# A tuned two-block transformer kernel: last tile in halves and quarters, a new order of the opening loads, and the final norm vector ahead of the power

## The reference

```python
def rms_norm(x, gain):
    y = xf * lax.rsqrt(jnp.mean(xf * xf, axis=-1, keepdims=True) + EPS)
    return y * gain

def swiglu_ffn(h, w_in, w_out):
    gate, up = jnp.split(h @ w_in, 2, axis=-1)
    return (jax.nn.silu(gate) * up) @ w_out

for l in range(DEPTH):                       # first block
    x = x + 0.5 * swiglu_ffn(rms_norm(x, ffn1_norm[l]), ffn1_w_in[l], ffn1_w_out[l])
    h = rms_norm(x, mix_norm[l])
    ...                                      # merged = gated sum of three mixers of h
    x = x + merged @ w_out[l]
    x = x + 0.5 * swiglu_ffn(rms_norm(x, ffn2_norm[l]), ffn2_w_in[l], ffn2_w_out[l])
...                                          # second block, gated residuals
return rms_norm(h, final_norm_g)
```

## Time and profile before

| | us |
|---|---|
| median of 3 runs | 3209.15 (3208.39 to 3211.18) |
| profiled execution, its own time | 3211.39 |
| profiled execution, span | 3209.5 |
| TensorE busy | 3144.4 (98%) |
| VectorE busy | 1989.4 (62%) |
| ScalarE busy | 1361.2 (42%) |
| mean granted TensorE clock | 0.996 of full |

### The profile page before, as it was taken

How to read it: one execution, slowest core, us unless ns; L and a number is a source line. 1 busy time by engine, 2 the same in 40 slices (tenths; PEclk the granted TensorE clock), 3 DMA queues, 4 the chain that set the end, 5 groups by cost and what they waited for, 6 DMA issues and landing times.

```text
span 3209.5 us, 39756 instructions
## 1 busy us (share of the span) xinstructions
PE 3144.4 (98%) x15550; PEld 2624.9 (82%) x15550; DVE 1989.4 (62%) x2775; ACT 1361.2 (42%) x1907; POOL 129.6 (4%) x160
## 2 busy tenths in 40 slices
PE   8999999999999999999999999999999999999998
PEld 7888888888888887888888888788887788887787
DVE  7968778788687787663344444776335642345665
ACT  6546655454566555323233333322223322245553
POOL 1000000000000000000000000300000000021000
PEclk9999999999999999999999999999999999999999
DMA  7755356666554576542332222254324633253354
GB/s 251 250 192 176 128 197 223 223 236 237 160 184 132 196 244 210 187 147 95 103 99 79 79 92 85 99 171 155 108 92 158 214 114 109 88 140 90 105 188 153
DMA packets 334901, 496.78 MB, mean 155 GB/s; under 512 B 11042, under 2 KB 221884, under 8 KB 334716
## 3 DMA queue, kind: packets, MB, share of 16 engines
q1 hardware_dynamic: 330652, 483.46, 45.5%
q0 software_dynamic: 4064, 10.77, 1.5%
HBM read 493.09 MB, written 1.10 MB: 154 GB/s over the span
## 4 chain that ended last, share of the span: by engine, by line
PE 94%; DVE 3%; issue 1%; ACT 1%; DMA 0%; POOL 0%; SPq 0%; DVEq 0%; POOLq 0%; ACTq 0%
PE bank L567 23%; PE bank L569 23%; PE bank L568 23%; PE bank L623 13%; PE bank L627 7%; PE bank L753 1%; PE bank L582 1%; PE bank L768 0%; PE bank L1047 0%; DVE wlo L1730 0%; DMA raw<-in_w_in_dram 0%; DVE bank L2565 0%; PE bank L590 0%; POOL small L2633 0%; ACT npr L1678 0%
## 5 line engine op out<-in xcount | busy, mean ns | idle before, releaser
L1730 DVE TENSOR_TENSOR wlo<-raw,whi 128x1024 fp32r<-128x1024 f32 (+1 forms) x780 | 940.2, 1213 | 900.6 <-ACT whi L1213 898.5
L1213 ACT ACTIVATE whi<-raw 128x1024 fp32r<-128x1024 f32 (+1 forms) x780 | 816.0, 1050 | 1154.4 <-PE bank L569 993.0
L567 PE MATMUL bank<-xTh,whi 128*128 128x512 f32 (+1 forms) x1312 | 508.8, 388 | 7.5 <-DVE xTl L1811 7.4
L568 PE MATMUL bank<-xTl,whi 128*128 128x512 f32 (+1 forms) x1312 | 504.6, 385 | 0.0
L569 PE MATMUL bank<-xTh,wlo 128*128 128x512 f32 (+1 forms) x1312 | 504.6, 385 | 0.0
L623 PE MATMUL bank<-xT,whi 128*128 128x512 f32 x1760 | 444.7, 395 | 2.2 <-DVE xT L1811 1.6
L567 PE MATMUL bank<-whi,hh 128*128 128x512 f32 x968 | 377.9, 390 | 0.0
L569 PE MATMUL bank<-whi,hl 128*128 128x512 f32 x968 | 376.8, 389 | 0.0
L568 PE MATMUL bank<-wlo,hh 128*128 128x512 f32 x968 | 376.6, 389 | 0.0
L623 PEld LDWEIGHTS bank<-xT,whi 128*128 128x128 f32 x1760 | 319.6, 190 | 64.1 <-issue 3.4
L567 PEld LDWEIGHTS bank<-xTh,whi 128*128 128x128 f32 x1312 | 247.1, 188 | 67.2 <-issue 16.5
(11 more groups left out here) (383 smaller groups left out, 3651.8 us busy)
## 6 DMA issues: line engine op xcount, KB each, us to landing
raw<-in_ffn_w_in_dram SPq DMA_DIRECT2D x176, 1024.0 KB, 5.2
raw<-in_ffn_w_out_dram SPq DMA_DIRECT2D x80, 1024.0 KB, 5.1
mraw<-in_w_mod_dram SPq DMA_DIRECT2D x72, 1024.0 KB, 5.0
raw<-in_w_in_dram SPq DMA_DIRECT2D x44, 1024.0 KB, 5.2
raw<-in_ret_w_in_dram SPq DMA_DIRECT2D x24, 1024.0 KB, 5.1
raw<-in_w_branch_dram SPq DMA_DIRECT2D x12, 1024.0 KB, 5.1
raw<-in_nat_w_qkv_dram SPq DMA_DIRECT2D x12, 1024.0 KB, 5.2
raw<-in_ffn_w_out_dram SPq DMA_DIRECT2D x16, 512.0 KB, 3.5
```

Source lines behind the costliest of these rows:

```text
L567: pe.matmul(ps, lh, rh, start=start, stop=False, skip_group_check=True)
L568: pe.matmul(ps, lh, rl, start=False, stop=False, skip_group_check=True)
L1213: nc.scalar.activation(hi, src, ACT.Copy).then_inc(*e.inc("hi", key, part))
L1730: nc.vector.tensor_tensor(lo, src, hi.bitcast(F32), ALU.subtract).then_inc(*e.inc("lo", key, part))
```

## The change

The residual's last tile is finished in pieces. For columns 512 to 1023 of the last tile, TensorE finishes the first 256 columns over the last slabs ("first"), then the other 256 in a bank of its own ("rest"), which starts from zero at those slabs. What the old bank already holds of the other 256 columns ("begun") is added to X while the rest is computed. So VectorE has three additions of 256 columns (gated: three pairs; at `rw`, where all k are in the halves, two) in place of one of 512. ScalarE squares only the first piece; `mean_begun` adds up, and VectorE squares the rest itself and adds it to the sum. The scaled row is written in quarters, three on VectorE and one on ScalarE, and each transpose waits for its quarter alone. VectorE's lo split of the next stage's first slab moves from ahead of the turned reads to behind the second of them (mixers) or the last (FFNs). The banks of the FFN's pairs are released by VectorE's sum alone.

At the opening X comes as two loads with no memset behind them; the identity comes alone, then the seven norm vectors, then the first slab, then the rest of the constants. VectorE rounds part 0 of the first slab, ScalarE part 1. At the end the rows are multiplied by the final norm vector first and by the root afterwards; the last scaling is shared by VectorE (640 columns) and ScalarE (384), and each tile is written in two pieces.

The diff, cut to its core:

```diff
+NEXT_T = {("mx", 0): 256, ("f1", 1): 256, ("mx", 1): 256, ("f2", 0): 256, ("f2", 1): 256, ("g1", 0): 256, ("r",): 512,
+          ("g2", 0): 512, ("g1", 1): 512, ("n",): 512, ("g2", 1): 256, ("last",): 256}
+def pieces_of_rows(name, t, n, whole=False):
+    if n == 0 or t != last_tile(name):
+        return [Piece(n)]
+    first = Piece(n, ("first",), (), 0, 256, True, whole)
+    begun = [] if whole else [Piece(n, ("begun",), (), 256, 256, False, True)]
+    return [first, *begun, Piece(n, ("rest",), ("rest",), 0, 256)]
+def scaled_by(name, t):
+    if name in (("f1", 0), ("last",)) or t != last_tile(name):
+        return (("dve", 0, 512), ("act", 512, 512))
+    return (("dve", 0, 256), ("dve", 256, 256), ("dve", 512, 256), ("act", 768, 256))
...
-            sp.dma_start(X[:, 0:2, :], w["x"][0].rearrange("(t p) n -> p t n", p=P))\
-              .then_inc(L.sem("x_landed"), 16)
-            sp.dma_start(cst[:, :], consts["cst"][:, 0:C_FLIP]).then_inc(L.sem("gains_landed"), 16)
-            slab_range(0, 1)
+            for t in range(2):
+                sp.dma_start(X[:, t, :], w["x"][0, t * P:(t + 1) * P, :]).then_inc(L.sem(f"x{t}_landed"), 16)
+                for n in range(2):
+                    L.events["X", ("f1", 0), t, n] = (f"x{t}_landed", 16)
+            sp.dma_start(cst[:, 0:P], consts["cst"][:, 0:P]).then_inc(L.sem("ident_landed"), 16)
             loads = list(row_loads())
             for dst, src in loads[:GAIN_LOADS]:
                 sp.dma_start(dst, src).then_inc(L.sem("gains_landed"), 16)
-            L.gains = 16 * (GAIN_LOADS + 1)
+            L.gains = 16 * GAIN_LOADS
+            slab_range(0, 1)
+            sp.dma_start(cst[:, P:C_FLIP], consts["cst"][:, P:C_FLIP]).then_inc(L.sem("cst_landed"), 16)
             slab_range(1, NRAW)
...
+                    if halved and t == tiles[-1]:
+                        columns(t, ps[t][:, 0:256], slice(0, 256), ("first",), k0, 0, False)
+                        rest = new(*name, t, "rest", ring=ring)
+                        columns(t, rest[:, 0:256], slice(256, 512), ("rest",), k0, k0, True)
+                    else:
+                        columns(t, ps[t][:, :], slice(0, 512), (), k0, 0, t == tiles[-1])
...
-                            pe.wait_ge(*e.at(*ready, t, half))
                             for k in ks:
+                                pe.wait_ge(*e.at("xn", name, t, scaled_part(name, t, k)))
...
+            def mean_begun(name, t):
+                dve.wait_ge(*e.at("ssa", name, t, 1))
+                link(STT(small[:, t:t + 1], small[:, t:t + 1], EPS, small[:, 4 + t:5 + t], ALU.add, ALU.add))
             def mean_square(name, t):
+                if name != ("f1", 0) and t == last_tile(name):
+                    dve.wait_ge(*e.at("X", name, t, 1, "rest"))
+                    a = X[:, t, 768:1024]
+                    V.tensor_tensor_reduce(junk_v[:, 0:256], a, a, 1.0 / D, small[:, t:t + 1], ALU.mult, ALU.add,
+                                           small[:, 12 + t:13 + t]).then_inc(*e.inc("ms", name, t))
+                    return
...
+                    if k == (1 if name[0] == "mx" else KD - 1):
+                        first_slab(until, name)
...
+                    for p in pieces_of_rows(nxt, t, n):
+                        if p.bank:
+                            before_rest()
+                        if p.waits:
+                            dve.wait_ge(*e.at("down", name, n, t, *p.key))
+                        if p.bank:
+                            dve.wait_ge(*e.at("X", nxt, t, n, "begun"))
+                        x, of = X[:, t, p.x], ("down", name, n, t, *p.bank)
+                        ps, frees = unit(*of)[:, p.ps], of if p.frees else None
+                        if not whos:
+                            STT(x, ps, 0.5, x, ALU.mult, ALU.add).then_inc(*e.inc("X", nxt, t, n, *p.key, frees=frees))
+                        else:
+                            y = sg[:, (t + len(p.bank)) % 2, p.ps]
+                            dve.wait_ge(*e.at("gb", name))
+                            TT(y, ps, gb[:, t // 2, p.x], ALU.mult).then_inc(*e.inc("sgg", name, n, t, *p.key, frees=frees))
+                            dve.wait_ge(*e.at("sgg", name, n, t, *p.key))
+                            TT(x, y, x, ALU.add).then_inc(*e.inc("X", nxt, t, n, *p.key))
...
             dve.wait_ge(L.sem("fg_landed"), 16)
-            for t in range(2):
-                for n in range(2):
-                    dve.wait_ge(*e.at("xn", ("last",), t, n))
-                TT(fo[:, t, :], xn[:, t, :], fg[:, :], ALU.mult).then_inc(*e.inc("out_row", t))
+            rows(0)
+            squares(nm, 0, 1)
+            mean_square(nm, 0)
+            by_gain(0, slice(0, D)).then_inc(*e.inc("by_gain", 0))
+            by_gain(1, slice(0, 512))
+            out_row(0)
+            rows(1, before_rest=before_rest)
+            dve.wait_ge(*e.at("X", nm, 1, 1, "rest"))
+            mean_square(nm, 1)
+            by_gain(1, slice(768, D)).then_inc(*e.inc("by_gain", 1))
+            out_row(1)
```

More of the change, by code:

```diff
@@ L702, in rows_by, with rows_by_tile, columns @@
                 return k0
[L704 to L711 removed]
+            def rows_by_tile(keys, name, ps, xh, xl, k0, total, ring="all", ahead_of_tile=lambda t: None, halved=False):
+                def columns(t, dst, c, key_of, k, clears, uses):
                     for key in keys:
@@ L1208, in until @@
                     split[0] += 1
+                    if i == 0:
+                        continue
                     src, hi, _ = part_views(key, part)
@@ L1237, in scaled @@
                     act.wait_ge(*e.at("rstd", name, t))
-                    A(stripe(xn, 1, t), stripe(X, 1, t), ACT.Copy, scale=small[:, 8 + t:9 + t])\
-                        .then_inc(*e.inc("xn", name, t, 1))
+                    if name == ("last",):
+                        act.wait_ge(*e.at("by_gain", t))
+                        A(fo[:, t, OUT[1]], fo[:, t, OUT[1]], ACT.Copy, scale=small[:, 8 + t:9 + t])\
+                            .then_inc(*e.inc("out_row", t, 1))
+                        return
+                    for i, (engine, c, n) in enumerate(scaled_by(name, t)):
+                        if engine == "act":
+                            A(xn[:, t, c:c + n], X[:, t, c:c + n], ACT.Copy, scale=small[:, 8 + t:9 + t])\
+                                .then_inc(*e.inc("xn", name, t, i))
+                if name == ("f1", 0):
+                    squares(name, 1, 1)
+                    for t in range(2):
+                        scaled(t)
+                    return
                 order, scales = tile_order(name, T), []
@@ L1774, in norm @@
             def norm(name, T, rows=None, tiles=4):
+                if name == ("f1", 0):
+                    squares(name, 0, 1)
+                    for t in range(2):
+                        mean_square(name, t)
+                    columns(0)
+                    for t in range(2):
+                        dve.wait_ge(*e.at("rstd", name, t))
+                        TS(stripe(xn, 0, t), stripe(X, 0, t), small[:, 8 + t:9 + t], None, ALU.mult)\
+                            .then_inc(*e.inc("xn", name, t, 0))
+                    key = slabs.items[0][0]
+                    src, hi, _ = part_views(key, 0)
+                    dve.wait_ge(*arrival(key))
+                    V.tensor_copy(hi, src).then_inc(*e.inc("hi", key, 0))
+                    dve.wait_ge(*e.at("cols_copied", 0))
+                    return
                 def scaled(t):
@@ L1789, in norm @@
                     if rows and t < tiles:
-                        rows(t)
+                        rows(t, before_rest=lambda: mean_begun(name, t))
                     if t % 2 == 0 and t < tiles:
@@ L1917, in summed @@
                    low.rearrange("p (m t) -> p m t", m=2), ALU.add).then_inc(*e.inc(stage, name, g))
-                L.freed[(part, name, g, 0)] = L.events[(stage, name, g)]
+                for mc in range(2):
+                    L.freed[(part, name, g, mc)] = L.events[(stage, name, g)]
             def short_hidden(name):
```

181 lines of the change are left out of this document (102 added, 79 removed).

## The result

The changed kernel takes 3214.34 us (median of 20 runs, 3212.05 to 3216.48) against 3209.12 for the kernel before (20 runs); the ratio is 1.0015 with a 95% interval of 1.0009 to 1.0021. It is about 5 us slower, less than the 0.2% that was set as the line, where 3209.3 was forecast and 3213.3 was the range's upper end. The profiled execution has a span of 3213.0 us, 3.5 over the span before; that of before lay some 2 us above its median, that of after did not. Times of single runs scatter by 5 us and more, so I place the loss by where TensorE's products stand in the traces.

The account below looks back on a forecast made before the run. TensorE, busy 98% of the span, was taken as the bound, so only its standstills could pay. The terms summed to +0.2 us: 3211.39 becomes 3211.6, the median 3209.3, with a range of 3203.3 to 3213.3.

Parts of the forecast that it names:

- Opening: Start of the kernel: vectors land at 8.2, first product at 13.1 and not 15.32; -2.0 us, bounds -3.3 and +1.0.
- into the second block: Boundary with 24 transposes: their first group waits for the rest's bank; +0.8 us, bounds 0 and 0.8.
- behind the retention: Boundary where VectorE is already late: the pieces put the scaling 0.85 later; +0.9 us, bounds 0 and 1.2.
- behind neighbourhood attention: Boundary: scaling 0.9 later, but two lo splits move behind the first xT; -0.5 us, bounds -1.2 and +0.5.
- plain boundaries: Ungated FFN into a 256-token stage: VectorE has slack, xT starts earlier; -0.55 us each for two, bounds 0 and -1.0.
- Mixer into ffn2: Two boundaries where VectorE is late: scaling starts 0.76 later; +0.7 us each, +1.4 for both, bounds 0 and 2.2 together.
- First mixer: First FFN into the first mixer: moved lo split delays slabs, boundary gain waited away again; +1.0 us, bounds -0.5 and +1.3.
- End: After the last product: rest's multiply starts 2.6 behind it, last scaling shared; -0.6 us, bounds -1.4 and +0.3.
- Rival 1: All boundaries: VectorE's pieces run ahead of the last matmul's end everywhere; -9.3 us, 3199.9; chance 0.07.
- Rival 2: Five half-clock stretches behind boundaries: shorter waits could remove all of them; 3202 us; chance 0.06.
- Rival 3: Boundaries: new waits for bank 2 or late pieces let the clock fall; four stretches +7.4, 3216.7 us; chance 0.04.
- Rival 4: Opening stays: the slab lands 8 us behind its issue, first product still at 15.3; 3211.3 us; chance 0.13.

Follow-up runs that it names:

- run 5: The changed kernel with GpSimd's 13 small loads held until the first slab's second half is split, near 16.6 us: 3210.97 us, ratio 1.0006.
- run 9: The changed kernel with GpSimd's 13 small loads held to about 34 us and the steps using them three groups later: 3205.93 us, ratio 0.9989.
- run 4: The changed kernel with the first slab issued ahead of the seven norm vectors, behind X and the identity: 3210.35 us, ratio 1.0007.
- Run 6: The changed kernel with the seven norm vectors issued by ScalarE's queue, SyncE going straight from identity to first slab: 3208.48 us, ratio 0.9997.
- run 1: The changed kernel with the opening of the kernel before; the tail pieces and the new end stay: 3208.16 us, ratio 1.0000.
- run 12: The kernel before with only its small loads moved to 34 us: 3207.83 us, ratio 0.9995.
- run 2: The kernel before with the new opening alone: 3214.85 us, ratio 1.0021.
- run 3: The changed kernel with TensorE's three transposes of the parameters one product pair later, no load moved: 3210.35 us, ratio 1.0004.
- Run 7: The changed kernel with the last tile whole into the second block and behind the retention, ScalarE alone scaling the first tile's last row: 3213.31 us, ratio 1.0012.
- run 10: The run 9 kernel with the last tile whole ahead of seven norms and ScalarE scaling all of the first tile's last row: 3204.55 us, ratio 0.9985.
- run 11: The changed kernel with the first slab's lo split ahead of the turned columns again in the two mixers: 3215.38 us in one profiled execution.

## Why the prediction failed

**Opening: the wrong step.** "The parameters (now behind the table's rest) may hold TensorE 0.2 at its next stop." They held it 7.10 us, and the clock took 2.6 more. The steps ahead of it came in time or sooner (vectors 8.2, measured 6.4; first slab rounded from 10.37; first product 13.1, measured 11.71), and that made the wait longer: TensorE came to the parameters 3.9 us sooner than in the kernel before. The vectors even broke my bound, "not before 7.8": it took X's 5.1 us for those of an idle queue, but the earlier trace rows are of a kernel that issues the table and the first slab within 1 us behind X. I followed the first slab past the vectors, but not the second and third slab, the parameters behind them, nor GpSimd's queue, whose 13 loads begin when the norm's two powers are done, and so moved by -1.9, while the first slab moved by +3.3. Runs 5 and 9 show that these packets are what made the third slab and the parameters late; run 4 shows that with the slab first the same small loads do no harm. Run 6 shows the same with another order of issues. So it takes both: the first slab's megabyte 3.3 us later, and the small loads beside what follows it. Whether it matters that the small loads themselves came 1.9 us sooner no run tells; none held them to 9.57. By the view of the first 32 us a packet of GpSimd's takes some 0.19 us of an engine (15.4% of 16 engines and 32 us, over 416 packets), one of SyncE's 0.06 (78.1% over 6654), though it holds more bytes. The 0.19 is no fixed price: the same 416 packets took 0.12 each in the kernel before (9.6%), 0.10 in runs 1 and 4 (7.9%), and 0.19 in run 12 (34.8% of 14 us from 35 on), where TensorE waited for none of it. Why they take longer in one kernel than in another is open.

The Trainium skill (DMA: Bandwidth & Descriptors, Queues, rings and completion order) has each engine take turns between the queues packet by packet. The shares of 77.3% and 33.0% above agree with slow packets taking turns with fast ones; no run here shows the order of single packets.

**The boundaries.** This table gives, in us, the gap between the end of the last product and the first product of the next stage; the old code is in the kernel before and runs 2 and 12, the new in the changed kernel and runs 1, 3 to 6 and 9. A range with a half-clock stretch at that place in some of the runs is marked with a star.

```
boundary                         old code        new code        stage ahead  net          forecast
first FFN -> mixer               4.56 to 4.57    3.79 to 3.81    +0.2         see below    +1.0
mixers -> ffn2 (two)             4.45 to 5.36*   4.83 to 5.75*   see below    +0.3, -0.2   +0.7 each
ffn2 -> ffn1, ffn1 -> mixer      4.50 to 4.56    3.68 to 3.80    +0.2         -0.6 each    -0.55 each
into the second block            5.66            6.10            not resolved +0.4         +0.8
gated, into 512 tokens (three)   6.38 to 6.40    6.30 to 6.32    +0.2         +0.1 each    +0.1 each
behind the retention             10.06 to 10.12  10.64 to 10.77  +0.1         +0.7         +0.9
behind neighbourhood attention   6.53 to 6.54    6.30 to 6.57*   not resolved -0.1         -0.5
last product to the span's end   9.07 to 9.09    9.05 to 9.06    -            0            -0.6
```

"Stage ahead" is how much longer the stage takes from first to last product for the split matmuls (one gated stage 365.11 against 364.87, the second ffn1 186.69 against 186.49): 0.20 to 0.24 where I had 0.33. With about 0 for the first mixer the net terms add up to about +0.2 where the forecast had +2.2 for them; run 1 says 0.0 with 3 us to either side. At the plain boundaries the forecast held to 0.05 to 0.2. The timeline into the second ffn1 in the changed kernel, beside the earlier trace rows:

```profile
648.15 1.07 PE L806 MATMUL bank<-cst,xn 128*128 128x128 f32 x8 [0.73 <-issue]
649.53 1.18 PE L806 MATMUL bank<-cst,xn 128*128 128x128 f32 x8 [0.32 <-DVE xn L1875]
651.10 3.08 PE L667 MATMUL bank<-xT,whi 128*128 128x512 f32 x12 [0.38 <-DVE xT L1917]
```

T2, the end of the last product, is 647.42 here (the prediction's T lies 0.15 ahead of that end, 642.47 against 642.62): the transposes of tile 0 start at T2+0.73, behind the rest's bank, as forecast, and the product at T2+3.68. The same bank costs where 24 transposes wait for it, into the second block (beside the earlier trace rows):

```profile
1275.72 3.69 PE L806 MATMUL bank<-cst,xn 128*128 128x128 f32 x32 [0.73 <-issue]
```

Run 7 undid the pieces there and behind the retention and got 5.66 and 10.06 back: shown, not only argued.

Three small terms failed. *Mixer into ffn2* (forecast +0.7 each, measured +0.3 and -0.2): the scaling did start late, as forecast (beside the earlier trace rows; first add of the last tile at 455.68, quarters at 458.76):

```profile
455.68 0.75 DVE L2491 TENSOR_TENSOR X<-bank,X 128x256 f32<-128x256 f32 x2
...
458.76 0.88 DVE L1875 TENSOR_SCALAR xn<-X,small 128x256 f32<-128x256 f32 x3 [0.67 <-POOL small L2766]
```

3.08 us pass between the two where the earlier trace rows have 2.31, and TensorE turns the first quarter 0.41 behind the start of its scaling where the half took 0.54: so far the term held. But the second mixer itself is 0.6 us shorter in every kernel with its last tile halved (240.51 in run 9, 240.55 changed; 241.15 before and 241.36 in run 10), which I had not seen coming. The trace shows where: the four kernels with the whole last tile (before, runs 2, 10 and 12) have this wait inside the second mixer (the line is of the kernel before), and none of the ten others has it.

```profile
953.87 0.47 PE L567 MATMUL bank<-whi,yth 128*128 128x512 f32 x1 [0.78 <-ACT st L1525]
```

The product waits for a bank that ScalarE is still reading into `st`; in the changed kernel it starts at 956.34, ahead of that read at 956.72. It takes its bank from the ring `short` (banks 0 to 3), and the rest of the first mixer's last tile has taken one more from that ring, so it gets the next one. That this shift is the cause is read from the program; no run shifts the ring alone. From first product to first product the first mixer with its boundary takes 248.27 in run 9 (halved) and 248.01 in run 10 (whole), the second 246.26 and 246.45. *First mixer* (forecast +1.0): from the end of the first FFN's last product to that of the mixer's last there pass 247.06 to 247.71 us in the three kernels with the old code (mean 247.4) and 246.92 to 247.73 in the ten with the new (mean 247.3). So most of the 0.77 gained at the boundary is lost again inside the mixer, as the prediction said that it would be; with the 0.2 of the stage ahead the sum is about 0. The 1 us more that the moved lo split was to cost did not come (run 11). *End:* the order that I read off held, VectorE comes to the pieces late, but it does so by more:

```profile
3202.14 1.47 POOL L2766 TENSOR_TENSOR small<-small,cols 128x1 f32<-128x1 f32 x1 [56.90 <-DVE small L1837]
```

```profile
3201.97 1.82 DVE L2728 TENSOR_TENSOR fo<-X,fg 128x1024 f32<-128x1024 f32 x2
3203.72 0.55 DVE L2733 TENSOR_SCALAR fo<-fo,small 128x640 f32<-128x640 f32 x1
...
3206.30 0.42 DVE L2086 TENSOR_TENSOR sg<-bank,gb 128x256 f32<-128x256 f32 x1
```

VectorE's rest multiply starts at 3206.30, 2.4 behind the last product (which ends at 3203.92; forecast 2.6), and the last scaling ends at 3209.22, 5.3 behind it, where `fo` was done 5.8 behind (3206.24 against 3200.42). So 0.5 was gained there and lost again by the writes: the span ends 3.8 behind the last scaling where it was 3.3, and 9.1 behind the last product in both. That the four writes are what takes 0.5 longer was not tried apart. With the first tile's scaling moved to ScalarE (run 7) it is 8.69.

**Rivals.** Rival 1 (3199.9) and 2 (3202) did not come: counted over the whole span in units of 3.4 us, the length of the shortest, the half-clock stretches between opening and end are 7, 8 and 7 in the three runs with the old boundaries and 6 to 9 in those with the new, and the same code keeps or loses the one at 453, 1648 or 2929 from run to run. (The prediction's five stretches in the kernel before leave out the one at 2979.8; the one behind the retention is two units long.) Rival 3 had the right kind of cost, a new wait with the half clock behind it, at the wrong place: not at boundaries, but in the opening. Rival 4 had the right place; its condition, the slab 8 us behind its issue, did not occur (5.3, from 5.03 to 10.37). The upper bound of +1.0 for the opening was taken from the first slab alone. What I had in hand for the parameters was a landing no later than 21.75, met by TensorE without a wait; setting that beside the arrival that I forecast myself, 2.2 us sooner (13.1 against 15.32), would have given a wait of up to 2.2 even with every load landing when it did; the 0.2 had no row behind it. And nothing in hand priced what happened on top: the loads landing 6 us later than they had.

## What to carry to other kernels

When a load is moved in a queue, follow every load behind it, to the last one that some engine waits for in the next 20 us, and the loads of the other queues whose start depends on the step that was made faster. A step that comes 4 us sooner only gains if all that it needs next comes sooner too: the wait that follows an early start is the one to price, with the clock that falls in it. Small loads with few bytes are not small work: put them where no large transfer is awaited. Cutting a tail into pieces pays where the engine that takes the pieces is idle when the tail comes, and costs where it is late or where the additional bank is wanted at once.

## What the runs showed of the hardware

- GpSimd's 13 loads with 0.23 MB in 416 packets took 15.4% of the 16 engines' time in the first 32 us of the changed kernel, 9.6% in the kernel before and 7.9% in run 4; from 17 to 19 us of the changed kernel 77.3%, at 100 GB/s in all. Issuing them 27 us later moved the products by 9.2 us (from 6.0 behind the kernel before to 3.2 ahead) and the median by 8 (3214.3 to 3205.9).
- Seven small loads on ScalarE's queue, issued beside a megabyte on SyncE's, landed at 10.1; issued on SyncE's ahead of it, at 6.4. The Trainium skill (DMA: Bandwidth & Descriptors, Issuing engines are not separate DMA queues) says that a second issuing engine saves only the time of issuing; run 6 agrees: the last vector was issued 2.0 us sooner than in run 4 (3.64 against 5.59), and the vectors landed 0.6 sooner.
- In run 3 standstills of 0.59 and 1.31 us, 0.4 apart, were followed by a stretch at half clock (1.2 GHz); single ones of 0.83 in run 5 and 0.73 in run 9 at the opening's parameters were not.
- GpSimd's power of 128x1 took 1.47 us beside a VectorE product of 1024 columns, at the end of each kernel with that order (3202.14 above, 3195.53 in run 1), and 0.56 in the kernel before. The cause was not tried apart.
